# A hybrid decoder step on one core: where the final state is turned, how the gate's products are packed, how a norm takes its root, and which row tile and query load come first

## What is computed

```python
# time mix, after the scan over time that gives y and the final state s_fin
yn = ((y - mu) * lax.rsqrt(var + LNX_EPS)).reshape(bq, t, d) * a_lnx_g + a_lnx_b
bonus = (jnp.sum(rh * kh * a_r_k, axis=-1, keepdims=True) * vh).reshape(bq, t, d)
g = jax.nn.sigmoid(xg @ a_g1) @ a_g2                  # inner width 160
out = ((yn + bonus) * g) @ a_w_o                      # s_fin is an output, too
# every sub-layer
x = layer_norm(ALPHA * x + h)                         # (x - mu) * rsqrt(var + LN_EPS) * g + b
# after layer 0's experts
kv_new = einsum('btd,dgsnh->btgsnh', x, b_w_kv)       # 1024 x 1536, shared by the attention
q = x @ b_w_q                                         # 1024 x 3072, three dilation groups
```

## Time and profile before

| | us |
|---|---|
| median of three runs | 1766.25 |
| lowest, highest | 1763.91, 1768.02 |
| the profiled execution | 1764.17 |
| its span | 1762.3 |
| PE busy | 1562.2 (89% of the span) |
| DVE, ACT, POOL busy | 579.9, 387.7, 194.3 |

### The profile page before, as it was taken

The page is one execution under the profiler, slowest core; times in us unless marked ns, Lnnn a source line. Parts: engine busy times, 40 slices in busy tenths (PEclk is TensorE's granted clock), DMA queues, the critical chain, the costliest instruction groups (busy, mean ns, idle before and its releaser), DMA issues. The chain is left out here.

```text
span 1762.3 us, 46279 instructions
## 1 busy us (share of the span) xinstructions
PE 1562.2 (89%) x20468; PEld 1150.9 (65%) x20468; DVE 579.9 (33%) x1502; ACT 387.7 (22%) x928; POOL 194.3 (11%) x190
## 2 busy tenths in 40 slices
PE   7999999996997799999669879999999589999970
PEld 6878868875675455555458768887878445555540
DVE  5121545663544312121181100005654512121217
ACT  1023334331522011110122001115652201110113
POOL 1000025643300300000010000000000020000002
PEclk8999999998988799999979989999999799999995
DMA  9400001011424999999951375552120699999973
GB/s 288 166 32 25 1 4 35 28 34 37 158 72 167 342 376 384 379 383 382 355 157 48 97 108 123 119 106 87 37 74 0 260 336 384 378 380 380 380 268 145
DMA packets 218132, 331.09 MB, mean 188 GB/s; under 512 B 70456, under 2 KB 117344, under 8 KB 217936
## 3 DMA queue, kind: packets, MB, share of 16 engines
q1 hardware_dynamic: 193552, 285.13, 47.2%
q0 software_dynamic: 8208, 25.57, 5.4%
q10 hardware_dynamic: 16176, 17.43, 2.9%
HBM read 295.73 MB, written 32.39 MB: 186 GB/s over the span
## 5 line engine op out<-in xcount | busy, mean ns | idle before, releaser
L2408 PE MATMUL bank<-x_early,ring 128*128 128x256 f32 (+1 forms) x768 | 175.5, 390 | 15.1 <-DMA ring<-in_b_w_q 11.3
L1945 PE MATMUL bank<-ring_extra,xT 128*32 128x256 f32 x3264 | 180.5, 379 | 0.0
L2408 PEld LDWEIGHTS bank<-x_early,ring 128*128 128x128 f32 x768 | 148.0, 194 | 38.7 <-DMA ring<-in_b_w_q 11.5
L1945 PE MATMUL bank<-ring,xT 128*32 128x256 f32 x2880 | 162.9, 385 | 1.3 <-DVE xT L1643 1.3
L1945 PEld LDWEIGHTS bank<-ring_extra,xT 128*32 128x32 f32 x3264 | 104.4, 110 | 70.0 <-issue 2.7
L1945 PEld LDWEIGHTS bank<-ring,xT 128*32 128x32 f32 x2880 | 92.3, 111 | 66.4 <-issue 5.9
L1648 DVE TENSOR_TENSOR sg<-sg,bank 128x128 f32<-128x128 f32 x96 | 27.1, 282 | 297.9 <-ACT sg L1816 297.9
L1963 PE MATMUL bank<-ring_extra,hT 128*32 128x256 f32 x1920 | 107.7, 380 | 2.6 <-DVE hT L1656 1.8
L1816 ACT ACTIVATE sg<-bank 128x128 f32<-128x128 f32 x96 | 26.7, 278 | 357.5 <-PE bank L1945 357.5
L376 PE MATMUL bank<-mix,ring 128*128 128x260 f32 x448 | 100.5, 384 | 0.0
L376 PEld LDWEIGHTS bank<-mix,ring 128*128 128x128 f32 x448 | 84.5, 190 | 15.3 <-ACT k L558 2.4
(11 more groups left out here) (408 smaller groups left out, 2377.2 us busy)
## 6 DMA issues: line engine op xcount, KB each, us to landing
ring_extra<-in_moe_w_down SPq DMA_DIRECT2D x40, 1024.0 KB, 15.1
ring_extra<-in_moe_w_gate SPq DMA_DIRECT2D x70, 512.0 KB, 9.4
ring_extra<-in_moe_w_up SPq DMA_DIRECT2D x70, 512.0 KB, 13.2
ring<-in_moe_w_gate SPq DMA_DIRECT2D x62, 512.0 KB, 9.7
ring<-in_moe_w_up SPq DMA_DIRECT2D x62, 512.0 KB, 12.7
ring<-in_moe_w_down SPq DMA_DIRECT2D x26, 1024.0 KB, 15.0
ring<-in_a_w_rkv SPq DMA_DIRECT2D x12, 1024.0 KB, 7.1
expert_out<-yo ACTq DMA_DIRECT2D x128, 96.0 KB, 6.4
```

The source lines that it names most:

```text
L1945: ins = pe.matmul(ps[u][32 * q:32 * q + 32, 0:256], xT[:, kt, 32 * u:32 * u + 32], gate_up(w, kt % 2, q), start=kt == 0, stop=kt == KT - 1)
L2408: ins = pe.matmul(ps[2 * (job % 3) + h][:, 0:n], w[:, kt_, rr, :], z[:, kt_, lo:lo + n], start=kt_ == 0, stop=kt_ == 7)
```

## The change

- **Chunks and gate.** The block between them is gone. PE turns the state at the end of the chunks' block, into banks 6 and 7; reading and turning the requests' rows, the copies and the state's store stand inside the gate's block.
- **Gate products.** `g2b` and `low_b` lie twice, on partitions 0 to 31 and 32 to 63. Both halves of `g2a` come first, then the two 32-row products on different rows of the array.
- **Roots in output_norm.** Reciprocal on DVE, then one Sqrt on ACT. The combining step of `expert_layer` keeps Ln and Exp.
- **K/V step.** Row tiles in the order 0, 4, 1, 2, 3; each tile is normalised right after its statistics. PE multiplies tile 0, then the requests (into the other banks), then tiles 1, 2, 3. The first two query chunks are issued after the second tile's rows are final, no longer ahead of the combining step.
- **Attention.** The third query chunk stands ahead of the wait for the bias copies, and every later one is one place earlier.

```diff
@@ time_mix_chunks, PE, behind the loop over chunks
+                pe.wait_ge(m_new, CHUNKS + 1)
+                for p in range(PAIRS):
+                    pe.transpose(ps[6 + p // 4][0:64, (p % 4) * 128:(p % 4) * 128 + 128], M[:, p], ident)
@@ time_mix_gate, SP
+                sp.dma_start(yrows, y_dram).then_inc(back, 16)
                 sp.dma_start(low_a, low_dram[0:128]).then_inc(low_in, 16)
-                sp.dma_start(low_b, low_dram[128:160]).then_inc(low_in, 16)
                 sp.dma_start(g2a, io["a_g2"][0, 0:128]).then_inc(low_in, 16)
-                sp.dma_start(g2b, io["a_g2"][0, 128:160]).then_inc(low_in, 16)
+                for h in range(2):
+                    sp.dma_start(low_b[32 * h:32 * h + 32], low_dram[128:160]).then_inc(low_in, 16)
+                    sp.dma_start(g2b[32 * h:32 * h + 32], io["a_g2"][0, 128:160]).then_inc(low_in, 16)
+                sp.wait_ge(copied, 2)
+                out = io["wkv_prompt"][0, 0].rearrange("h i j -> i h j")
+                sp.dma_start(out, Sout.rearrange("i q (e j) -> i (q e) j", e=2)).then_inc(stored, 16)
+                sp.wait_ge(stored, 16)
+                sp.wait_ge(y_in, 1)
                 feed.upto(sp, 0, TIME_OUT_END)
@@ time_mix_gate, PE
-                    for h in range(2):
-                        o = ps[2 * gate_pair(kt) + h][:, 0:HALF]
-                        pe.matmul(o, g2a[:, cols], low_a[:, half(h)], start=True, stop=False)
-                        ins = pe.matmul(o, g2b[:, cols], low_b[:, half(h)], start=False, stop=True)
-                    ins.then_inc(gated, 1)
+                    for h in range(2):
+                        pe.matmul(o[h], g2a[:, cols], low_a[:, half(h)], start=True, stop=False)
+                    for h in range(2):
+                        own_rows = slice(32 * h, 32 * h + 32)
+                        pe.matmul(o[h], g2b[own_rows, cols], low_b[own_rows, half(h)], start=False, stop=True).then_inc(gated, 1)
+
+                pe.wait_ge(back, 16)
+                for kt in range(KT):
+                    ins = pe.transpose(ps[4][:, kt * 8:kt * 8 + 8], yrows[:, kt * 128:(kt + 1) * 128], core.c("ident")[0:REQ, 0:REQ])
+                ins.then_inc(turned, 1)
+                pe.wait_ge(y_in, 1)
@@ time_mix_gate, DVE, ahead of its loop
+                dve.wait_ge(turned, 1)
+                dve.tensor_copy(y[:, :, SEQ:ROWS], ps[4][:, 0:64].rearrange("p (k r) -> p k r", k=KT)).then_inc(y_in, 1)
+                for b in range(2):
+                    dve.tensor_copy(Sout[:, 4 * b:4 * b + 4], ps[6 + b][0:64, :].rearrange("p (q s) -> p q s", q=4)).then_inc(copied, 1)
@@ output_norm, DVE and ACT
                     dve.tensor_scalar(mv[0:n, t, 3:4], mv[0:n, t, 1:2], LN_EPS, None, ALU.add).then_inc(ag, 1)
+                    dve.wait_ge(ag, 3 * i + 2)
+                    dve.reciprocal(mv[0:n, t, 3:4], mv[0:n, t, 3:4]).then_inc(ag, 1)
...
-                    act.activation(mv[0:n, t, 2:3], mv[0:n, t, 3:4], ACT.Ln).then_inc(root, 1)
-                    act.wait_ge(root, 2 * i + 1)
-                    act.activation(mv[0:n, t, 2:3], mv[0:n, t, 2:3], ACT.Exp, scale=-0.5).then_inc(root, 1)
+                    act.activation(mv[0:n, t, 2:3], mv[0:n, t, 3:4], ACT.Sqrt).then_inc(root, 1)
@@ expert_layer
-        order = (4, 0, 1, 2, 3) if kv else range(TILES)
+        order = (0, 4, 1, 2, 3) if kv else range(TILES)
@@ expert_layer, DVE
                 if kv:
                     kF, v0 = kv
+                    for i in range(TILES):
+                        statistics(i)
+                        normalise(i)
+                    keep_keys(0, 0)
                     add_requests()
@@ expert_layer, SP
                 feed.upto(sp, 6 * EXPERTS, next_stop, every)
-                if kv:
-                    feed.upto(sp, 6 * EXPERTS, next_stop + len(QUERY_SLOTS), QUERY_SLOTS)
...
+                    if kv and i == 1:
+                        feed.upto(sp, 6 * EXPERTS, next_stop + len(QUERY_SLOTS), QUERY_SLOTS)
@@ attention, SP
-                feed.upto(sp, 12, KV_END + 2, QUERY_SLOTS)
+                feed.upto(sp, 12, KV_END + 3, QUERY_SLOTS)
                 sp.wait_ge(bias.stored, 48)
                 for n in range(KVH):
                     for l in range(2):
                         bias.load(sp, landed[n // 2], n, l)
-                        feed.upto(sp, 12, KV_END + 3 + 2 * n + l, QUERY_SLOTS)
+                        feed.upto(sp, 12, KV_END + 4 + 2 * n + l, QUERY_SLOTS)
```

159 lines of the change are left out of this document (68 added, 91 removed).

## The result

| | before | changed |
|---|---|---|
| median, us | 1766.73 (4 runs) | 1739.82 (4 runs) |
| lowest, highest | 1763.91, 1768.02 | 1732.34, 1741.14 |
| profiled execution, span | 1764.17, 1762.3 | 1740.63, 1738.4 |

The changed kernel is faster: ratio 0.9841, 95% interval 0.981 to 0.9872. The medians differ by 26.9 us; in a second set of runs of the same two kernels, by 27.1 (1764.45 and 1737.33, ratio 0.9835, 0.9817 to 0.9853). The forecast was 1736.5 and a sum of 28.4.

A forecast was written before the change was run, and what follows sets the result against it. PE, busy 89% of the span, was taken as the bound, so gains are shortened chains PE waits for: 4.0 + 5.2 + 3.5 + 3.5 + 12.2 = 28.4 us off 1764.2, giving 1735.8, adjusted to 1736.5; range 1728 to 1746 (8 in 10).

The forecast's parts named there:

- A1: Border between chunks and gate: first centre product comes earlier after the state's transposes; 4.0 us gained (range 3 to 4.5).
- A2: Gate loop and DVE's tail: 3.0 us from shorter gates 2 to 4, 2.2 from the tail; 5.2 (range 2.5 to 6).
- B: Roots in output_norm: DVE's wait at the last tile goes in both layers; 3.5 us gained (range 2 to 3.7).
- C: K/V products: with tile 0 first, the row products effectively begin earlier; 3.5 us gained (range 0 to 5).
- D: Third query chunk issued ahead of the wait for the bias copies: 12.2 us gained (range 7.7 to 14.2).
- 1.1 for the rest of the slow clock: K/V products: 1.1 us allowed for remaining half-clock work once the row products begin.
- first of its two bounding cases: Third query chunk waits entirely for the bias copies and reaches PE at 1036.6, a wait of 3.6 us.
- (a): Third query chunk starves behind the bias copies and PE's clock falls: gain there 7.7, time 1741 us; chance 0.15.
- (b): K/V step: tile 0 first gives nothing, as full gathers land 3 to 4 us later; 1740 us; chance 0.12.
- (c): Gate: the 32-row products do not run together; the loop loses 1.3, DVE's tail nothing; 1738 us; chance 0.04.
- (d): Slower than before: half clock after the gate persists through output_norm's row tiles, 56 us more, 1792 us; chance 0.03.
- (e): Two terms, one the third chunk's, are covered by something unseen: within 0.2% of before; chance 0.02.

The follow-up runs named there:

- warm_kv: Changed kernel plus unread identity products in two idle places of PE, after the first gathered tile lands and behind the last turned keys; 1730.81 us, ratio 0.9812.
- early_bias: Changed kernel with the bias products between the halves of the first query job instead of behind it; 1734.64 us, ratio 0.9847.
- undo_kv: Changed kernel with the whole combining and K/V step of the kernel before (tile order 4, 0, 1, 2, 3); 1739.94 us, ratio 0.9878.
- best: Changed kernel plus unread products at K/V, first queries and output_norm's last tile, bias products inside the first query job, one Sqrt in the combining step; 1733.67 us.
- undo_gate: Changed kernel with the gate's products in the old order, both 32-row products on the same rows; 1739.7 us, ratio 0.9881.
- the second set: Changed kernel unedited (1737.33 us), with the separate state block (1740.82), with unread products in three places (1735.9); kernel before with gate packing alone (1760.02).

## Why the forecast was right, and where it was off

By the means of the table the parts give:

| part | forecast | measured | from |
|---|---|---|---|
| A1 border | 4.0 | 3.7 | 9.72 - 6.03 |
| A2 gate | 5.2 | 5.2 | 55.65 (two profiles) - 50.44 (nine) |
| B roots | 3.5 | 3.5 | 67.98 - 66.35 and 67.84 - 66.00 |
| C tile 0 first | 3.5 | 2.0 | 118.63 - 116.11, less 37.86 - 37.30 |
| D third chunk | 12.2 | 12.4 | 21.77 - 9.38 |
| sum | 28.4 | 26.8 | |

The sum agrees with 26.9 and 27.1 between the medians. That it does so within 0.3 us is partly luck: G0, G1 and the stretches without an edit are not in it, and they scatter by more. The five ranges of the forecast add up to 1731.5 to 1750, not to its 1729 to 1742; the measured 1739.82 is in both.

- **A1** was right step by step: the transposes lie under the store of step_out, and the first centre product is ruled by the 1.95 us from SP's issue (430.15) to PE (432.10).
- **A2** was right in size and in its first half: gates of 1.61 us (forecast 1.5), the second gate waits longer (0.93, was 0.48; forecast 1.4). The sum there counts 1.0 for each of gates 2 to 4, though it had worked out 0.9 a line before; measured are 0.81, or 2.4 for the three. The second half, the 2.2 us of DVE's tail, was read from one execution and is not a constant: the same kernel's second profile has 1.43, and without the packing the changed kernel has none. With both edits the stage is 5.2 shorter; the packing's own part is 2.6 (taken from the changed kernel) to 4.9 (put into the one before, against the mean of two profiles). The forecast gave all 5.2 to the packing, so that the two numbers are equal is in part luck. With half of PE's busy time at half clock taken off as above, A2 is 47.9 to 48.3 in the three kernels without the packing and 43.5 to 44.5 in the eleven with it. By this estimate the packing is worth some 4 us in either kernel, and the rest is where the clock fell.
- **B** was right in both layers. In the combining step, where Ln and Exp stay, the trace shows what is saved. Timeline of ACT, changed kernel:

```profile
901.76 1.28 ACT L1853 ACT_TABLE_LOAD   x1
...
903.30 0.20 ACT L1853 ACTIVATE mv<-mv 128x1 f32<-128x1 f32 x1 [0.26 <-DVE mv L1697]
903.52 1.28 ACT L1855 ACT_TABLE_LOAD   x1
904.81 0.20 ACT L1855 ACTIVATE mv<-mv 128x1 f32<-128x1 f32 x1
```

  Each of the two functions has a load of 1.28 us of its own. The first runs ahead of its activation's wait, the second can't. By the Trainium skill (ScalarE: Activation LUTs, Table sets: the hidden batching unit) Ln followed by Exp needs one load, since one set has both; here the program holds two, so that the whole pair costs what the trace says and not what the page would have.
- **C** is the term that was mis-sized. Its chain was right up to the first row product, 17.2 us after the gather. The step that failed is "1.1 for the rest of the slow clock": half clock lasted 5.0 us into the first 32 row passes and cost 2.45 there, and the first query job lost another 0.6 on average. Over the kernels, PE's busy time at half clock in C is 4.3 us on average with the old order (four kernels) and 6.4 with the new one (seven). With half of it taken off, C is 116.5 and 112.9: the order is worth 3.6, of which the clock takes back 1.1 in C and 0.6 in Q. With PE kept busy ahead of both places (warm_kv) C and Q are 4.1 us shorter, which shows that the clock is the cause.
- **D** was right within 0.2. The first of its two bounding cases happened, the chunk goes behind the copies, but it was milder than its price: a wait of 1.5 to 1.8 us instead of 3.6. Three of the four DMAs had been issued by 1017, when the first packet moved, and all had landed some 6 us later. PE's clock did not fall in so short a gap. early_bias removes the rest.
- **Rivals.** (a) was half right: the chunk starved behind the copies, but the clock did not fall, and D is 12.4 and not 7.7. (b) fell, since undo_kv costs 2.0 in C and Q; (c) fell with the 0.64 us for the packed pair. (d) fell: output_norm's row tiles take 13.98 to 14.08 each, as before (14.08). (e) fell.

## What to carry to other kernels

Sum the chains that end at the bottleneck engine, but price every piece of work that this engine does right after an idle stretch at half clock, and ask which work stands there after the change: putting the large products first also puts them into the slow stretch. Where a stretch at half clock begins and ends differs by a microsecond or two from profile to profile, so take a gain that hangs on it from several profiles, and take half of the busy time at half clock off before you compare stages. Unread products helped here where they ended about when the data came and work followed at once; where they ended late they became the wait, and ahead of a phase change they gave nothing.

## What the runs showed of the hardware beyond that

- A load that was issued while copies kept the DMA engines 0.95 busy at some 90 GB/s did not move until these were nearly done: 1 MB issued at 1007.5 was moved at up to 250 GB/s from 1017 on, and SP's own issue of it took 11.5 us instead of 3.2. In the eight kernels with the early chunk and the copies in their old place, the first packet came 9.3 to 9.6 us after the issue. With earlier copies it was 5.7 (early_bias) and 7.3 (best).
- Two 32-row products on different rows of PE's array run together: 0.64 us for both halves (464.12 to 464.76 above). In the old order each of the two took 0.64 by itself, for half as many passes (450.34 - 449.70 in undo_gate).
- In all four kernels of the second set, and in the profile shown of the changed kernel, PE stopped between pass 44 and 60 of the first expert's products, for 0.2 to 1.5 us at a time and in both layers; in the nine other profiles it ran through with the same or nearly the same programs. The DMA engines are 0.6 to 1.1 busy there, and a packet of the instruction queue (16 KB) passes in that stretch with and without the stops. What PE waits for was not found.
